# Both streams of the first feed-forward and of the key units in one matmul of 512 columns

## The chip, the cores and the metric

The kernel runs on one NeuronCore of a Trainium2 chip. The metric is the device time of one execution in microseconds (us); lower is better. Engines are named TensorE (PE in the rows, PEld for its weight loads), VectorE (DVE), ScalarE (ACT), GpSimd (POOL) and SyncE (SP).

## The reference

Two layers of a diffusion backbone work on 256 latent tokens and, in the first layer up to the attention, on 256 context tokens, each with 1024 features. What the change touches is the first feed-forward, which both streams pass with the same weights, and the keys of the attention, which both streams need:

```python
D_MODEL = 1024
SEQ = 256
...
CTX_LEN = 256
D_FF = 2816
...
def half_step_ffn(x, g_pre, g_post, shift, scale, gate, w_gate, w_up, w_down):
    h = modulated_norm(x, g_pre, shift, scale)
    y = (jax.nn.silu(h @ w_gate) * (h @ w_up)) @ w_down
    return x + FFN_RES * gate * rms_norm(y, g_post)

...
m_lat = (jax.nn.silu(c) @ w_mod[i] + b_mod[i]).reshape(b, N_MOD, 1, D_MODEL)
m_ctx = (jax.nn.silu(c_ctx) @ w_mod[i] + b_mod[i]).reshape(N_MOD, D_MODEL)
x = half_step_ffn(x, g[0], g[1], m_lat[:, 0], m_lat[:, 1], m_lat[:, 2],
                  ffn_w_gate[i, 0], ffn_w_up[i, 0], ffn_w_down[i, 0])
...
if keep_ctx:
    ctx = half_step_ffn(ctx, g[0], g[1], m_ctx[0], m_ctx[1], m_ctx[2],
                        ffn_w_gate[i, 0], ffn_w_up[i, 0], ffn_w_down[i, 0])
```

The last lines stand in the loop over the layers i, ahead of the token mixing; `keep_ctx` holds in layer 0 alone. The products `silu(c) @ w_mod` are matrix-vector products with 37.7 MB of weights for each layer; the kernel spreads them over the feed-forwards as "modulation jobs".

## The kernel before

**Layout and precision.** Features lie on the 128 partitions, tokens along the free dimension: `h` of a stream is 128 x 8 x 256 (`KT` = 8 blocks of features). Each fp32 operand is split into a rounded part and a rest (`hi`, `lo`, type float32r), and `product` (L1370 to L1374) issues three matmuls: w_hi x_hi (L1372), w_hi x_lo (L1373), w_lo x_hi (L1374). One weight unit is 128 x 1024 and makes one tile of 128 outputs: 8 blocks, 24 matmuls.

**Weight stream.** SyncE loads the units in order into 3 raw buffers. ScalarE copies each to `whi` (L434), VectorE subtracts into `wlo` (L801); both are rings of 6 units. The split of unit u + 6 waits until TensorE is done with unit u (`pe_done`).

**The first feed-forward** is 11 turns over six units each: gate and up of a tile pair s = 0, gate and up of pair s = 1, and two down units. Turns 0 and 10 are written out, 1 to 5 and 6 to 9 are loops. In a turn TensorE multiplies the four gate and up units with both streams. The latent gate and up of a pair share PSUM bank `gu[:, 0]` (gate in columns 0 to 255, up in 256 to 511), those of the context share `gu[:, 1]`. Order in a turn (`both_turn` of TensorE, L1512): (0, latent) (0, context) (1, latent) (1, context) (2, latent) (2, context), `job_sum(t)`, (3, latent) (3, context), then the two down products of the latent stream, then `job_sum(t + 1)`. Turn 0 takes both latent tiles of its first pair before the context's. After an odd latent tile the semaphore `lat_pair` rises; after each context tile `pe_done`.

ScalarE then applies SiLU to the gate half (L540), VectorE multiplies by the up half (L998). The latent result `act` is split for the down product: ScalarE `act_hi` (L544), VectorE `act_lo` (L1003). The context result goes to `act_ctx` and its down product comes after the turns, from `wstream` once more ("context down").

**Modulation jobs.** Two a turn. VectorE does a job in 8 steps, each a 128 x 512 weight block times a scalar of c, added to `part` (L816 the first, L818 the others). ScalarE rounds the total (`total_hi`, L537), VectorE subtracts (`total_lo`, L828, after a small copy to `hot`, L826), and TensorE sums over the partitions with two matmuls (`job_sum`, L1394 and L1396), for which it waits on `total_done`. All engines work strictly in the order of the program. VectorE's is set by a table in its `both_turn` (L1051): steps 0 to 3 at k = 0, 4 to 7 at k = 1, 8 to 11 at k = 2, 12 to 14 at k = 3, 15 at k = 4; each k ends with the split of unit u + k + 6, k = 2 begins with `job_lo(t)`, k = 4 ends with `job_lo(t + 1)`. At k = 1 and 3 the steps stand between the latent multiplication, `act_lo` and the context multiplication.

**After the turns** VectorE copies the latent result out of PSUM (L1140), for which the first context down product waits (`y_copied`). Later come the projection units of the attention. Units 16 to 19 are the keys, of both streams: `column_unit` once for the latent half and once for the context half of a bank, which ScalarE copies out (L659).

## Time and profile before

| | us |
|---|---|
| median of 3 runs | 1490.08 (1487.72 to 1493.79) |
| span of the profiled execution | 1499.0 |
| TensorE busy | 1434.4 (96%) |
| VectorE busy | 979.7 (65%) |
| ScalarE busy | 621.3 (41%) |
| GpSimd busy | 121.2 (8%) |
| the first feed-forward's turns | 53 to 392 us of the span |

The profiled execution is one run; its span is 8.9 us longer than the median of the runs, so a sum made from its rows is a sum of differences. A row of the timeline has start, duration, engine, line of the kernel, operation and operands; in brackets stands how long the engine was idle before it and what ended that. Matmuls are pipelined: their duration (0.28 us for 256 columns) is longer than the distance from one start to the next, so speed is read from starts. The granted clock is 1.00 at TensorE's upper level, 2.4 GHz, and 0.50 at the lower, 1.2 GHz.

### The profile page before, as it was taken

The numbers are of one execution on the slowest core, as the hardware profiler recorded it, in microseconds if no ns is written. First come the engines' busy times: TensorE is split into PE (matmuls) and PEld (weight loads), VectorE is DVE, ScalarE is ACT, GpSimd is POOL, SyncE is SP. The second block draws the span as 40 slices with busy tenths as digits, with TensorE's granted clock in tenths as the row PEclk, the third lists the DMA queues.
The fourth block names the chain that finished last, engine by engine and source line by source line (L and its number), as shares of the span: only waits on it lengthen the run. The fifth ranks groups of instructions, "written<-read, shape, count | busy, mean of one in ns | idle before, by whom it ended". The sixth has DMA issues, their size and how long they took to land.

```text
span 1499.0 us, 27870 instructions
## 1 busy us (share of the span) xinstructions
PE 1434.4 (96%) x10570; PEld 1310.5 (87%) x10570; DVE 979.7 (65%) x1425; ACT 621.3 (41%) x951; POOL 121.2 (8%) x200
## 2 busy tenths in 40 slices
PE   7899999999999999999999999999999989999997
PEld 2699999999899976589999989999876878899996
DVE  2677677777676824458787878755685785755554
ACT  2433232323465623345444455444435432544442
POOL 2000001111004002101111101100000020000000
PEclk9999999999999988999999999999999998999999
DMA  8455547777557532038888857856432432266651
GB/s 331 155 182 186 179 154 225 240 250 238 176 162 186 159 92 74 11 115 260 288 303 289 291 181 243 281 180 185 149 113 62 150 127 84 77 192 182 182 176 48
DMA packets 74482, 268.26 MB, mean 179 GB/s; under 512 B 9018, under 2 KB 9573, under 8 KB 73840
## 3 DMA queue, kind: packets, MB, share of 16 engines
q1 hardware_dynamic: 52128, 187.03, 38.4%
q0 software_dynamic: 22288, 80.30, 16.8%
q8 instruction: 47, 0.77, 0.2%
q14 instruction: 19, 0.16, 0.0%
HBM read 266.25 MB, written 1.05 MB: 178 GB/s over the span
## 4 chain that ended last, share of the span: by engine, by line
PE 68%; DVE 13%; issue 7%; ACT 6%; DMA 6%; DVEq 0%; ACTq 0%; SPq 0%; POOL 0%; POOLq 0%
PE gu L1372 13%; PE gu L1374 13%; PE gu L1373 13%; PE acc L1372 5%; PE acc L1374 5%; PE acc L1373 5%; DMA raw<-in_wstream_dram 5%; DVE wlo L801 4%; ACT whi L434 4%; PE mean_p L1414 2%; DVE part L818 1%; PE acc L1640 1%; DVE rstd L866 1%; PE gu L1481 1%; PE acc L1757 1%
## 5 line engine op out<-in xcount | busy, mean ns | idle before, releaser
L801 DVE TENSOR_TENSOR wlo<-raw,whi 128x1024 fp32r<-128x1024 f32 x350 | 432.9, 1242 | 284.4 <-ACT whi L434 282.9
L1372 PE MATMUL gu<-h_lat_hi,whi 128*128 128x256 f32 x1760 | 506.8, 288 | 11.6 <-DVE h_lat_lo L910 4.1
L434 ACT ACTIVATE whi<-raw 128x1024 fp32r<-128x1024 f32 x350 | 366.8, 1053 | 333.6 <-PE gu L1374 144.2
L1373 PE MATMUL gu<-h_lat_lo,whi 128*128 128x256 f32 x1760 | 500.1, 284 | 0.0
L1374 PE MATMUL gu<-h_lat_hi,wlo 128*128 128x256 f32 x1760 | 500.0, 284 | 0.0
L1372 PEld LDWEIGHTS gu<-h_lat_hi,whi 128*128 128x128 f32 x1760 | 339.8, 193 | 29.5 <-issue 17.7
L1373 PEld LDWEIGHTS gu<-h_lat_lo,whi 128*128 128x128 f32 x1760 | 340.0, 193 | 2.3 <-issue 1.7
L1374 PEld LDWEIGHTS gu<-h_lat_hi,wlo 128*128 128x128 f32 x1760 | 339.9, 193 | 0.0
L1372 PE MATMUL acc<-act_hi,whi 128*128 128x256 f32 x880 | 250.8, 285 | 3.3 <-DVE z L1140 2.6
L1373 PE MATMUL acc<-act_lo,whi 128*128 128x256 f32 x880 | 249.6, 284 | 0.0
L1374 PE MATMUL acc<-act_hi,wlo 128*128 128x256 f32 x880 | 249.5, 284 | 0.0
L818 DVE SCALAR_TENSOR_TENSOR part<-wm,cvec,part 128x512 f32<-128x512 f32 x266 | 199.3, 749 | 5.4
L1372 PEld LDWEIGHTS acc<-act_hi,whi 128*128 128x128 f32 x880 | 169.3, 192 | 6.2 <-DVE act_lo L1131 3.3
L1373 PEld LDWEIGHTS acc<-act_lo,whi 128*128 128x128 f32 x880 | 169.4, 193 | 0.0
L1374 PEld LDWEIGHTS acc<-act_hi,wlo 128*128 128x128 f32 x880 | 169.4, 193 | 0.0
L356 POOL DMA_DIRECT2D wm<-in_wmod_dram x136 | 71.9, 529 | 598.0 <-DVE part L818 577.9
L540 ACT ACTIVATE gated<-gu 128x256 f32<-128x256 f32 x110 | 41.9, 381 | 166.9 <-PE gu L1374 166.9
L1372 PE MATMUL gu<-h_ctx_hi,whi 128*128 128x256 f32 x384 | 108.7, 283 | 1.3 <-DVE area L998 1.3
L1373 PE MATMUL gu<-h_ctx_lo,whi 128*128 128x256 f32 x384 | 108.7, 283 | 0.0
L1374 PE MATMUL gu<-h_ctx_hi,wlo 128*128 128x256 f32 x384 | 108.6, 283 | 0.0
L998 DVE TENSOR_TENSOR act<-gated,gu 128x256 f32<-128x256 f32 x88 | 36.8, 419 | 61.5 <-ACT gated L540 61.2
L1372 PEld LDWEIGHTS gu<-h_ctx_hi,whi 128*128 128x128 f32 x384 | 73.7, 192 | 1.5 <-DVE wlo L801 1.5
(193 smaller groups left out, 1466.2 us busy)
## 6 DMA issues: line engine op xcount, KB each, us to landing
raw<-in_wstream_dram SPq DMA_DIRECT2D x350, 512.0 KB, 4.0
wm<-in_wmod_dram POOLq DMA_DIRECT2D x136, 512.0 KB, 5.1
area<-in_wmod_dram POOLq DMA_DIRECT2D x8, 512.0 KB, 8.0
area<-in_rpb_dram POOLq DMA_DIRECT2D x32, 64.0 KB, 3.1
x_lat<-in_x_in_dram SPq DMA_DIRECT2D x1, 1024.0 KB, 8.6
area<-in_ctx_in_dram SPq DMA_DIRECT2D x1, 1024.0 KB, 12.0
area<-in_dft_in_dram POOLq DMA_DIRECT2D x1, 1024.0 KB, 8.3
area<-in_window_in_dram POOLq DMA_DIRECT2D x1, 1024.0 KB, 11.4
```

The lines of the kernel that those rows point to most:

```text
L356: pool.dma_start(dst[:, 2 * part_:2 * part_ + 2, :], src[:, 2 * part_:2 * part_ + 2, :]).then_inc(sems[part_ // 2], 16)
L434: nc.scalar.activation(whi[:, phase % RING, :], raw[:, phase % RAW, :], ACT.Copy).then_inc(hi_done, 1)
L540: nc.scalar.activation(gated[:, s, :], gu[:, s, 0:T], ACT.Silu).then_inc(silu_done, 1)
L801: nc.vector.tensor_tensor(wlo[:, u.base % RING, :], raw[:, u.base % RAW, :], whi[:, u.base % RING, :].bitcast(F32), ALU.subtract).then_inc ...
L818: ins = nc.vector.scalar_tensor_tensor(out=part[:, :], in0=wm[:, kt, :], scalar=c, in1=part[:, :], op0=ALU.mult, op1=ALU.add)
L866: nc.vector.reciprocal(rstd[:, :], root[:, :]).then_inc(rstd_done, 1)
L998: nc.vector.tensor_tensor(dst, gated[:, s, :], gu[:, s, T:2 * T], ALU.mult).then_inc(act_mul, 1)
L1372: nc.tensor.matmul(out_, w_hi, x_hi, start=start, stop=False, skip_group_check=True)
L1373: nc.tensor.matmul(out_, w_hi, x_lo, start=False, stop=False, skip_group_check=True)
L1374: return nc.tensor.matmul(out_, w_lo, x_hi, start=False, stop=stop, skip_group_check=True)
L1414: ins = nc.tensor.matmul(mean_p[:, 0:T], mean_mat[:, :], sq[:, m, :], start=(m == 0), stop=(m == KT - 1))
L1481: ins = nc.tensor.matmul([job_p, gu[:, 0, :]][l % 2][0:2, :], cvec[:, kt, :], src[:, kt, :], start=(kt == 0), stop=(kt == KT - 1))
```

## The change

The two streams' `h` move into one tensor of 128 x 8 x 2 x 256, so that a feature block of both streams is one run of 512 columns. Bank `gu[:, 0]` now holds the gate of both streams, `gu[:, 1]` the up of both. From turn 1 on (and for the second pair of turn 0) a weight block is multiplied with both streams in one matmul of 512 columns. ScalarE applies SiLU to 512 columns at once, after the gate tile. VectorE waits for the up tile's `pe_done`, multiplies for the latent and then for the context stream, does `act_lo`, and then the job steps of that k. The semaphore `lat_pair` is gone. The key units take one matmul of 512 columns in place of two of 256.

```diff
@@ tensors
-        h_hi = [sb("h_lat_hi", [P, KT, T], F32R), sb("h_ctx_hi", [P, KT, T], F32R)]
-        h_lo = [sb("h_lat_lo", [P, KT, T], F32R), sb("h_ctx_lo", [P, KT, T], F32R)]
+        both_hi = sb("h_hi", [P, KT, 2, T], F32R)
+        both_lo = sb("h_lo", [P, KT, 2, T], F32R)
+        h_hi = [both_hi[:, :, s, :] for s in (LAT, CTX)]
+        h_lo = [both_lo[:, :, s, :] for s in (LAT, CTX)]
@@ ScalarE
+            def both_turn(u, n, ft, t):
+
+                for k in range(6):
+                    s = (k // 2) % 2
+                    if k in (0, 2):
+                        a.wait_ge(pe_done, at_unit(u, k + 1))
+                        if not (isinstance(ft, int) and ft + s == 0):
+                            a.wait_ge(act_mul, 2 * s + n)
+                        nc.scalar.activation(gated[:, :, :].rearrange("p a b -> p (a b)"), gu[:, 0, :],
+                                             ACT.Silu).then_inc(silu_done, 1)
+                    if k in (1, 3):
+                        a.wait_ge(act_mul, 2 * s + n + 1)
+                        nc.scalar.activation(act_hi[:, s, :], act[:, s, :], ACT.Copy).then_inc(act_hi_done, 1)
+                    split(u.plus(k + RING))
+                    if k in (1, 4):
+                        job_hi(t if k == 1 else t + 1)
@@ VectorE, both_turn
-                def latent(s, ops):
-                    gate_up(n + 2 * s, 0, act[:, s, :])
-                    for x in ops[:2]:
-                        op(x)
-                    act_los(n + 2 * s, ft + s, s)
-                    for x in ops[2:]:
-                        op(x)
-
-                first = isinstance(i, int) and i == 0
                 for k in range(6):
                     s = (k // 2) % 2
                     ops = plan.get(k, ())
-                    if k == 0 and first:
-                        latent(0, ops)
-                    elif k in (1, 3):
-                        if not (k == 1 and first):
-                            latent(s, ops)
+                    if k == 2:
+                        job_lo(t, r)
+                    if k in (1, 3):
+                        v.wait_ge(silu_done, ft + (s + 1))
+                        v.wait_ge(pe_done, at_unit(u, k + 1))
+                        nc.vector.tensor_tensor(act[:, s, :], gated[:, 0, :], gu[:, 1, 0:T], ALU.mult).then_inc(act_mul, 1)
                         dst = act_ctx[:, ft + s, :] if isinstance(ft, int) \
                             else act_ctx[:, bass.ds(ft + s, 1), :].rearrange("p a b -> p (a b)")
-                        gate_up(n + (2 * s + 1), 1, dst)
...
+                        nc.vector.tensor_tensor(dst, gated[:, 1, :], gu[:, 1, T:2 * T], ALU.mult).then_inc(act_mul, 1)
+                        act_los(n + 2 * s, ft + s, s)
+                    for x in ops:
+                        op(x)
                     split(u.plus(k + RING))
@@ TensorE, both_turn
+                def tile(k):
+                    s = k // 2
+                    pe.wait_ge(lo_done, at_unit(u.plus(k), 1))
+                    if k % 2 == 0:
+                        pe.wait_ge(silu_done, ft + s)
+                    else:
+                        pe.wait_ge(act_mul, n + 2 * s)
+                    for kt in range(KT):
+                        ins = product(gu[:, k % 2, :], *wblock(u.plus(k), kt), both_hi[:, kt, :, :], both_lo[:, kt, :, :],
+                                      kt == 0, kt == KT - 1)
+                    ins.then_inc(pe_done, 1)
+
+                if first:
+                    for k, stream in ((0, LAT), (1, LAT), (0, CTX), (1, CTX)):
+                        stream_tile(k, stream)
+                else:
+                    tile(0)
+                    tile(1)
+                tile(2)
                 job_sum(t, first)
-                tile(3, LAT)
-                tile(3, CTX)
+                tile(3)
@@ TensorE, key units
-                column_unit(Unit(U_AB + idx), gu[:, idx % 2, 0:T], lat, last=False)
-                column_unit(Unit(U_AB + idx), gu[:, idx % 2, T:2 * T], con)
+                column_unit(Unit(U_AB + idx), gu[:, idx % 2, :], (both_hi, both_lo))
```

`stream_tile`, used for the first pair of turn 0 alone, is the old tile of one stream with the new places in the banks. The table of the job steps is the same.

What this does to the order of the instructions is best seen on VectorE. First its first pair in a turn, up to the job that TensorE's first `job_sum` waits for (turn 10, which is written out; L998, L1003, L818, L801, L828 of before are L1069 and L1072, L1005, L820, L803, L830 of after). Before:

```order
L998 TENSOR_TENSOR act<-gated,gu 128x256 [waits silu_done]
L818 SCALAR_TENSOR_TENSOR part<-wm,cvec,part 128x512 [waits gemv_step,wm_landed1]
L818 SCALAR_TENSOR_TENSOR part<-wm,cvec,part 128x512 [waits gemv_step]
L1003 TENSOR_TENSOR act_lo<-act,act_hi 128x256 [waits act_mul,act_hi_done]
L818 SCALAR_TENSOR_TENSOR part<-wm,cvec,part 128x512 [waits gemv_step] x2
L998 TENSOR_TENSOR area<-gated,gu 128x256 [waits silu_done]
L801 TENSOR_TENSOR wlo<-raw,whi 128x1024 [waits hi_done]
L826 CAST hot<-one_in 128x22 [waits total_hi_done]
L828 TENSOR_TENSOR total_lo<-part,total_hi 128x512
```

The same place on VectorE after the change:

```order
L1069 TENSOR_TENSOR act<-gated,gu 128x256 [waits pe_done,silu_done]
L1072 TENSOR_TENSOR area<-gated,gu 128x256
L1005 TENSOR_TENSOR act_lo<-act,act_hi 128x256 [waits act_mul,act_hi_done]
L820 SCALAR_TENSOR_TENSOR part<-wm,cvec,part 128x512 [waits gemv_step,wm_landed1]
L820 SCALAR_TENSOR_TENSOR part<-wm,cvec,part 128x512 [waits gemv_step] x3
L803 TENSOR_TENSOR wlo<-raw,whi 128x1024 [waits hi_done]
L828 CAST hot<-one_in 128x22 [waits total_hi_done]
L830 TENSOR_TENSOR total_lo<-part,total_hi 128x512
```

The two job steps that stood ahead of `act_lo`, and the two ahead of the context's multiplication, now stand behind both multiplications and `act_lo`, and the first multiplication waits for `pe_done` of the up tile.

Next, on VectorE, the second pair of the same turn, up to the job of the last `job_sum`. Before:

```order
L998 TENSOR_TENSOR act<-gated,gu 128x256 [waits silu_done]
L818 SCALAR_TENSOR_TENSOR part<-wm,cvec,part 128x512 [waits gemv_step,wm_landed1]
L818 SCALAR_TENSOR_TENSOR part<-wm,cvec,part 128x512 [waits gemv_step]
L1003 TENSOR_TENSOR act_lo<-act,act_hi 128x256 [waits act_mul,act_hi_done]
L818 SCALAR_TENSOR_TENSOR part<-wm,cvec,part 128x512 [waits gemv_step]
L998 TENSOR_TENSOR area<-gated,gu 128x256 [waits silu_done]
L801 TENSOR_TENSOR wlo<-raw,whi 128x1024 [waits hi_done]
L818 SCALAR_TENSOR_TENSOR part<-wm,cvec,part 128x512 [waits gemv_step]
L801 TENSOR_TENSOR wlo<-raw,whi 128x1024 [waits hi_done]
L826 CAST hot<-one_in 128x22 [waits total_hi_done]
L828 TENSOR_TENSOR total_lo<-part,total_hi 128x512
```

After, on the same engine:

```order
L1069 TENSOR_TENSOR act<-gated,gu 128x256 [waits pe_done,silu_done]
L1072 TENSOR_TENSOR area<-gated,gu 128x256
L1005 TENSOR_TENSOR act_lo<-act,act_hi 128x256 [waits act_mul,act_hi_done]
L820 SCALAR_TENSOR_TENSOR part<-wm,cvec,part 128x512 [waits gemv_step,wm_landed1]
L820 SCALAR_TENSOR_TENSOR part<-wm,cvec,part 128x512 [waits gemv_step] x2
L803 TENSOR_TENSOR wlo<-raw,whi 128x1024 [waits hi_done]
L820 SCALAR_TENSOR_TENSOR part<-wm,cvec,part 128x512 [waits gemv_step]
L803 TENSOR_TENSOR wlo<-raw,whi 128x1024 [waits hi_done]
L828 CAST hot<-one_in 128x22 [waits total_hi_done]
L830 TENSOR_TENSOR total_lo<-part,total_hi 128x512
```

Here three job steps move behind the multiplications in the same way; what follows them is unchanged. On TensorE `job_sum` keeps its place between tiles 2 and 3 and at the turn's end.

## Rows read from the trace of the kernel before

**Rows 1.** From 60 to 360 us: PE, PEld, DVE, ACT, POOL busy, clock, DMA.

```profile
60.00:360.00 300.00, 294.57 (x2392) 286.53 (x2391) 220.65 (x326) 98.69 (x145) 29.43 (x56) 1.00 0.62 201
```

**Rows 2.** Waits of TensorE, 60 to 392 us: total, times, longest.

```profile
PE job_p L1394 <- DVE total_lo L828: 4.1, 12, 1.6
```

**Rows 3.** Timeline of TensorE (start, duration, line, operation): 256 and 512 columns.

```profile
362.13 0.28 PE L1372 MATMUL gu<-h_lat_hi,whi 128*128 128x256 f32 x1
...
367.88 0.28 PE L1372 MATMUL gu<-h_lat_hi,whi 128*128 128x256 f32 x1
...
575.75 0.39 PE L1622 MATMUL acc<-whi,h_lat_hi 128*128 128x512 f32 x1
...
583.23 0.39 PE L1622 MATMUL acc<-whi,h_ctx_hi 128*128 128x512 f32 x1
```

**Rows 4.** Timeline of TensorE: start of turn 1, end of turn 2, start of turn 3.

```profile
89.66 0.28 PE L1372 MATMUL gu<-h_lat_hi,whi 128*128 128x256 f32 x1
...
149.59 0.41 PE L1394 MATMUL job_p<-total_hi,hot 128*22 128x512 f32 x1 [0.21 <-DVE total_lo L828]
150.16 0.38 PE L1372 MATMUL gu<-h_lat_hi,whi 128*128 128x256 f32 x1
```

**Rows 5.** Timeline of VectorE in turn 3, first pair and its job.

```profile
159.51 0.42 DVE L998 TENSOR_TENSOR act<-gated,gu 128x256 f32<-128x256 f32 x1 [0.98 <-ACT gated L540]
...
161.30 0.42 DVE L1003 TENSOR_TENSOR act_lo<-act,act_hi 128x256 fp32r<-128x256 f32 x1
161.64 1.53 DVE L818 SCALAR_TENSOR_TENSOR part<-wm,cvec,part 128x512 f32<-128x512 f32 x2
...
163.42 1.22 DVE L801 TENSOR_TENSOR wlo<-raw,whi 128x1024 fp32r<-128x1024 f32 x1
...
164.63 0.69 DVE L828 TENSOR_TENSOR total_lo<-part,total_hi 128x512 fp32r<-128x512 f32 x1
```

**Rows 6.** Timeline of VectorE in turn 3, second pair and its job.

```profile
171.49 0.42 DVE L998 TENSOR_TENSOR act<-gated,gu 128x256 f32<-128x256 f32 x1 [1.44 <-ACT gated L540]
...
177.92 1.23 DVE L801 TENSOR_TENSOR wlo<-raw,whi 128x1024 fp32r<-128x1024 f32 x1 [0.72 <-ACT whi L434]
...
179.14 0.68 DVE L828 TENSOR_TENSOR total_lo<-part,total_hi 128x512 fp32r<-128x512 f32 x1
```

**Rows 7.** Timeline of ScalarE in turn 3.

```profile
159.97 0.42 ACT L544 ACTIVATE act_hi<-act 128x256 fp32r<-128x256 f32 x1 [0.49 <-DVE act L998]
...
177.79 0.61 ACT L537 ACTIVATE total_hi<-part 128x512 fp32r<-128x512 f32 x1
```

**Rows 8.** Timeline of VectorE, then TensorE, in turn 0.

```profile
67.02 0.41 DVE L998 TENSOR_TENSOR act<-gated,gu 128x256 f32<-128x256 f32 x1
...
71.79 3.11 DVE L818 SCALAR_TENSOR_TENSOR part<-wm,cvec,part 128x512 f32<-128x512 f32 x4
...
76.82 0.49 DVE L816 TENSOR_SCALAR part<-wm,cvec 128x512 f32<-128x512 f32 x1
...
67.58 0.36 PE L1372 MATMUL gu<-h_lat_hi,whi 128*128 128x256 f32 x1 [0.47 <-DVE act L998]
...
76.77 0.41 PE L1394 MATMUL job_p<-total_hi,hot 128*22 128x512 f32 x1 [1.64 <-DVE total_lo L828]
...
77.25 0.28 PE L1372 MATMUL gu<-h_lat_hi,whi 128*128 128x256 f32 x1
```

**Rows 9.** End of turn 10: VectorE, then TensorE.

```profile
391.07 0.69 DVE L828 TENSOR_TENSOR total_lo<-part,total_hi 128x512 fp32r<-128x512 f32 x1
...
392.72 1.23 DVE L801 TENSOR_TENSOR wlo<-raw,whi 128x1024 fp32r<-128x1024 f32 x1 [0.96 <-ACT whi L434]
...
395.03 0.36 PE L1372 MATMUL acc<-act_hi,whi 128*128 128x256 f32 x1 [2.57 <-DVE z L1140]
```

**Rows 10.** Short stretches, as rows 1; third number from the end: granted clock.

```profile
76.00:78.00 2.00, 1.23 (x9) 1.06 (x10) 1.86 (x5) 0.51 (x1) 0.00 (x0) 1.00 0.27 25
...
396.00:400.00 4.00, 4.00 (x21) 3.88 (x20) 1.12 (x3) 2.42 (x6) 0.00 (x0) 0.57 0.28 111
```

More of the change, by code:

```diff
@@ L285, in program @@
         total_split, total_done = sem("total_hi_done"), sem("total_lo_done")
-        lat_pair, y_copied = sem("latent_pair_done"), sem("y_copied")
+        y_copied = sem("y_copied")
         cs_ready = sem("cs_ready")
@@ L1513, in both_turn, with stream_tile @@
                 t = i * 2 + T_AHEAD
-                def tile(k, stream):
-                    s = (k // 2) % 2
-                    uk = u.plus(k)
-                    if stream == LAT or first:
-                        pe.wait_ge(lo_done, at_unit(uk, 1))
-                    if k % 2 == 0 and not (first and k == 0):
-                        pe.wait_ge(act_mul, n + (2 * s + stream - 1))
+                def stream_tile(k, stream):
+                    if stream == LAT:
+                        pe.wait_ge(lo_done, at_unit(u.plus(k), 1))
                     for kt in range(KT):
-                        if first and k == 0 and kt % 2 == 0:
+                        if k == 0 and kt % 2 == 0:
                             pe.wait_ge(h_ready, 4 * stream + kt // 2 + 1)
-                        ins = product(gu[:, stream, (k % 2) * T:(k % 2) * T + T], *wblock(uk, kt),
+                        ins = product(gu[:, k, stream * T:stream * T + T], *wblock(u.plus(k), kt),
                                       h_hi[stream][:, kt, :], h_lo[stream][:, kt, :], kt == 0, kt == KT - 1)
@@ L1528, in tile @@
                         ins.then_inc(pe_done, 1)
-                    elif k % 2:
-                        ins.then_inc(lat_pair, 1)
-                start = [(0, LAT), (1, LAT), (0, CTX), (1, CTX)] if first else \
-                    [(0, LAT), (0, CTX), (1, LAT), (1, CTX)]
-                for k, stream in start + [(2, LAT), (2, CTX)]:
-                    tile(k, stream)
+                def tile(k):
+                    s = k // 2
+                    pe.wait_ge(lo_done, at_unit(u.plus(k), 1))
+                    if k % 2 == 0:
[13 more added lines that the diff above has]
+                tile(2)
                 job_sum(t, first)
-                tile(3, LAT)
-                tile(3, CTX)
+                tile(3)
                 for s in range(2):
```

39 lines of the change are left out of this document (8 added, 31 removed).

## The prediction, made before the changed kernel was run

> **What bounds the kernel now.** I read the chain of waits first: TensorE's products of this one helper carry it. Then I read the stretch that the change touches, the loop of the first feed-forward. From 60 to 360 us TensorE is busy for 294.57 of 300 us at a granted clock of 1.00, VectorE for 220.65 [rows 1]. From the waits of TensorE in the same stretch the reader should take one name: what it waits for is `total_lo`, the last step of a modulation job on VectorE, 12 times and 4.1 us in all [rows 2]. So TensorE's stream sets the pace, but one chain of VectorE lies directly beneath it. VectorE is idle a quarter of the time, and an idle share tells nothing of whether its work lies in the right place.
>
> A turn lasts 30.27 us: the first product of turn 1 starts at 89.66 and that of turn 10 at 362.13, nine turns [rows 3, 4].
>
> **What the wide matmul saves.** 48 matmuls of 256 columns take from 362.13 to 367.88, so 0.1198 us from start to start [rows 3]. 512 columns with weights of the same size are in the trace too, in the projection of the values: 33 of them from 575.75 to 583.23, 0.2267 us each [rows 3]. A pair of narrow ones becomes one wide one, 0.2396 against 0.2267: 0.0129 us saved. A weight tile of both streams (24 wide matmuls) takes 5.44 us in place of 5.75. Ten turns of four tiles, two tiles in turn 0 and the four key units make 46 tiles, 1104 pairs, 14.2 us of TensorE time.
>
> The Trainium skill (TensorE: Matmul & The Clock Gate, "Wait — 56ns, not 53.3ns?") has 215.7 ns from start to start for 512 columns and a fixed 2.5 ns for each matmul. The trace does not agree: it shows 226.7 ns for 512 [rows 3]. By the page the three tiles that stand in a turn's path below would be 0.79 us shorter, and the whole sum +3.9 us instead of +12.3 (the nine turns, tile 3 of turn 0 and the key units).
>
> **What the change moves.** Before, the latent stream had its own bank with gate and up; its half of a pair was complete 2.87 us before the context half, and SiLU, multiplication and split of it ran beneath the context's matmuls. VectorE got two job steps done between. Now the up tile of both streams ends at one moment. VectorE waits there for `pe_done`, multiplies twice, waits for ScalarE's `act_hi`, subtracts, and only then come the job steps, which are queued behind that wait. TensorE, one tile later, waits for the job's `total_lo`. I put the clock at zero at the first matmul of a steady turn.
>
> *First half.* Gate and up tile of pair 0: 2 x 5.44 = 10.88. The last matmul ends 0.39 - 0.23 = 0.16 later [rows 3]; I take 0.10 for the signal: 0.04 lies between a multiplication's end and `act_hi` (159.51 + 0.42 against 159.97) [rows 5, 7], and the loop's waits on registers may add a little (estimate). VectorE multiplies at 11.14. ScalarE's `act_hi` starts 0.46 later (159.51 to 159.97) and takes 0.42 [rows 5, 7], so with 0.04 for the signal the subtraction starts at 12.06; the second multiplication fits beneath. The next instruction starts 0.34 after it (161.30 to 161.64) [rows 5]: 12.40. Four job steps take 3.11, less 0.08 that neighbours overlap, 3.03 [rows 8]: 15.43. Split of a unit and `hot`: from 163.42 to 164.63, 1.21 [rows 5]: 16.64. `total_lo` 0.69 [rows 5] and 0.05 to the matmul (the same kind of signal): 17.38. ScalarE's `total_hi`, 0.61 [rows 7], lies beneath the split. TensorE is done with tile 2 at 16.32 and would go on at 16.44. It waits 0.94 us.
>
> *Second half.* From the job's first matmul to the next tile 0.48 (76.77 to 77.25) [rows 8]: tile 3 from 17.86 to 23.30. The same 0.16 + 0.10: 23.56. To the first job step 0.92 + 0.34: 24.82. Three steps 2.24: 27.06 (four steps less one of 0.79). Split 1.15 (1.23 less 0.08 [rows 6]): 28.21. The last job step, 0.75 less 0.08: 28.88. Split and `hot` 1.22 (177.92 to 179.14) [rows 6]: 30.10. `total_lo` and signal: 30.84. TensorE has finished both down products at 23.30 + 5.75 = 29.05, and waits 1.67 us behind the 0.12 of passage. Then 0.57 to the first matmul of the next turn (149.59 to 150.16) [rows 4]: 31.41.
>
> The wait of before at this place, 0.21 us [rows 4], had another cause: VectorE was 0.72 us idle there for ScalarE's `whi` [rows 6], which waited for the first down product. That cause is gone; VectorE's own queue takes its place.
>
> So a turn takes 31.4 in place of 30.27, **+1.14 us, nine times: +10.3 us.** The 1.24 us that a turn's wide matmuls save are spent, and as much again.
>
> *Turn 0.* It has no latent half ahead of VectorE's splits. Before, VectorE is done with them at 67.02 [rows 8]. Now follow four job steps, the first a plain product of 0.49 and not 0.75 [rows 8], so 2.76, to 69.78; split 1.15; then the chain as above: 1.26, 3.03, 1.21, 0.74, to 77.17. Before, the job matmul started at 76.77 [rows 8]: +0.4. The old waits of 0.47 and 1.34 us before tile 2 are gone, but all of that gain is waited for in front of the job. From there to turn 1: 13.9 (31.41 - 17.38, less 0.1 for the loop's branch) against 12.89 (76.77 to 89.66) [rows 4, 8]: +1.0. Together +1.4 us.
>
> *The clock in turn 0.* Tile 2 now starts at 66.95 and its last matmul ends at 72.55, so TensorE is idle for 4.6 us. The trace shows the granted clock after 2.57 us of idle time before 395.03: a mean of 0.58 from 396 to 400, so most of it at the lower of the two levels, 1.2 GHz, which costs 4 x 0.42 = 1.7 us [rows 9, 10]. After 1.64 us of idle time before 76.77 it stayed at 1.00 [rows 8, 10]. So 4.6 us will let it fall, once: **+1.7 us**.
>
> *Turn 10 and after.* Its `total_lo` ends 1.0 us later than before, counted from its start (30.7, against 391.07 + 0.69 - 362.13 = 29.63) [rows 3, 9]. Behind it VectorE was idle for 0.96 us for ScalarE's `whi`, which waited for the second down product [rows 9]; that product is now long done. So the copies of the latent result, for which TensorE waits until 395.03, come 1.0 us sooner after `total_lo`. Sum +0.1 us.
>
> *The key units.* Four tiles, 96 pairs, with nothing behind them on VectorE but splits: -1.2 us, whole on the path. ScalarE copies the finished bank beneath the next unit as before. One SiLU of 512 columns in place of two of 256, and the two-part rows of h, lie on engines with idle time: nothing, unless ScalarE were late for a split, and `total_hi` above has 0.6 us to spare. The weight stream keeps three raw buffers and the same order; the turn becomes longer, so the transfers have more time.
>
> **Sum:** +10.3 + 1.4 + 1.7 + 0.1 - 1.2 = +12.3 us. The profiled execution's span is 1499.0, 8.9 above the median 1490.1 of the runs; every term is a difference of a few us, so I add it to the median: **1502.4 us.**
>
> **Rivals.**
>
> *TensorE stays the bound (faster).* Place: the first `job_sum` and the second of each turn. It decides at the first half's chain, 6.50 us from the up tile's end (10.88) to the job's matmul (17.38), against 5.56 of tile 2 with its passage; the second needs 7.54 (23.30 to 30.84) against 5.87. If VectorE needed 0.94 us less in the one and 1.67 in the other, the whole 14.2 us would come, and most of turn 0's waits: 1475 us. The order of VectorE's instructions speaks against it, as does that the old chain had nothing left at the end of a turn (the wait of 0.21). 4%.
>
> *The chains are shorter than I make them, or the clock does not fall in turn 0.* Half the signal times and no fall give +8 to +3: 1493 to 1498. The terms are sums of starts in the same loop, so an error of 0.3 us in a turn is as much as I allow. 10%.
>
> *The clock falls in every turn.* The idle stretch at each turn's end is 1.6 us and one of 0.9 lies 12 us before it. If each such stretch brought 1.7 us at the lower clock, nine or ten times, the time would be 1519. Against it: 1.64 us in turn 0 did not let it fall [rows 8, 10]; for it: the new one is as long, ten times over, and 2.57 sufficed. 9%. The Trainium skill (same page, "A second HAM failure mode: psum-queue depth-cycling") tells of a kernel of 512-column matmuls going round PSUM banks whose short idle times made the clock swing; no row here shows it for idle times this short.
>
> *The wide matmul does not do what it says.* If 512 columns of h as the moving side took twice 0.1198, the three tiles in a turn's path would be 0.31 longer each: +8.4 us, and the key units' 1.2 lost: 1512. The only row of 512 has the weight matrix as the moving side. 3%.
>
> **How the numbers follow.** Forecast 74%, its own range 1498 to 1507 (0.3 us a turn each way, and the clock). The range of 1494 to 1511 takes in most of the shorter chains and a clock that falls in a few turns. 0.5% is 7.5 us, about what a measurement can tell here. Faster by more: 5%. Within it: 13%, the shorter chains. Slower: 82%.
>
> **What would show it.** In the changed kernel the waits of TensorE for `total_lo` should rise from 4.1 to about 31 us in this stretch, some 0.9 and 1.6 us by turns, and the first of them near 4.6. The turn should read 31.4 us. VectorE should show its idle time before the first multiplication of a pair and none from there to `total_lo`. The granted clock should dip once near 76 to 82 us. Wrong would be: no waits at `job_sum` (rival one), a clock below 1.00 throughout the stretch (rival three), wide matmuls 0.24 us apart (rival four).

## The result and the profile after

The changed kernel takes 1508.94 us (median of 4 runs, 1504.10 to 1515.68) against 1491.44 (1487.72 to 1493.79) of the kernel before on the same chip: a ratio of 1.0108, 95% interval 1.0081 to 1.0136, or 16.1 us more (12.1 to 20.3) by that ratio; the two medians lie 17.5 us apart. Predicted were 12.3 us more. A second measurement on another chip (`changed_again`, below) gave 1.0127 (1.0081 to 1.0173).

The busy time of each engine over the same stretch as [rows 1] and the waits of TensorE as in [rows 2]. Columns of the first: stretch, length, busy time and count of PE, PEld, DVE, ACT, POOL, granted clock, DMA share, GB/s.

```profile
60.00:360.00 300.00, 273.32 (x1402) 227.75 (x1401) 206.33 (x306) 88.61 (x118) 26.41 (x50) 0.98 0.56 189
75.00:83.00 8.00, 4.64 (x12) 3.47 (x13) 7.15 (x10) 2.06 (x3) 1.05 (x2) 0.57 0.40 115
284.00:288.00 4.00, 4.00 (x12) 3.18 (x11) 2.73 (x5) 0.00 (x0) 1.05 (x2) 0.57 0.96 329
```

The waits of TensorE for `total_lo` from 60 to 420 us, to the end of turn 10 as in [rows 2] (engine, line, what it waited for: total us, times, longest):

```profile
PE job_p L1383 <- DVE total_lo L830: 31.7, 22, 4.7
```

TensorE's busy time fell by 21 us in 300, and that is not work saved: the engine stands still instead, for 26.7 us of the 300. What it waits for is one name, `total_lo`, 31.7 us in place of 4.1. The two short stretches of a lower clock are new.

TensorE's timeline: turn 0's first job, the start of turn 1, the second job of turn 1 and both jobs of turn 2 (start, duration, line, operands; in brackets the idle time and what ended it):

```profile
73.26 0.39 PE L1363 MATMUL gu<-h_hi,wlo 128*128 128x512 f32 x1
78.36 0.62 PE L1383 MATMUL job_p<-total_hi,hot 128*22 128x512 f32 x1 [4.71 <-DVE total_lo L830]
...
94.31 0.39 PE L1361 MATMUL gu<-h_hi,whi 128*128 128x512 f32 x1
94.54 0.39 PE L1362 MATMUL gu<-h_lo,whi 128*128 128x512 f32 x1
94.76 0.39 PE L1363 MATMUL gu<-h_hi,wlo 128*128 128x512 f32 x1
...
125.20 0.41 PE L1383 MATMUL job_p<-total_hi,hot 128*22 128x512 f32 x1 [1.62 <-DVE total_lo L830]
...
143.33 0.41 PE L1383 MATMUL job_p<-total_hi,hot 128*22 128x512 f32 x1 [0.93 <-DVE total_lo L830]
...
156.78 0.41 PE L1383 MATMUL job_p<-total_hi,hot 128*22 128x512 f32 x1 [1.61 <-DVE total_lo L830]
157.03 0.40 PE L1385 MATMUL job_p<-total_lo,hot 128*22 128x512 f32 x1
157.34 0.49 PE L1361 MATMUL gu<-h_hi,whi 128*128 128x512 f32 x1
157.68 0.40 PE L1362 MATMUL gu<-h_lo,whi 128*128 128x512 f32 x1
```

The wide matmuls do start 0.227 us apart (94.31, 94.54, 94.76), as [rows 3] had it for other operands. In turns 1 to 9 the first job waits 0.92 to 0.93 us and the second 1.61 to 1.62. A turn lasts 31.6 us (125.20 to 156.78, the second jobs of turns 1 and 2) against 30.27.

VectorE in turn 2, first pair, to set beside [rows 5]:

```profile
133.22 1.22 DVE L803 TENSOR_TENSOR wlo<-raw,whi 128x1024 fp32r<-128x1024 f32 x1 [4.18 <-ACT whi L436]
137.00 0.42 DVE L1069 TENSOR_TENSOR act<-gated,gu 128x256 f32<-128x256 f32 x1 [2.55 <-PE gu L1363]
137.33 0.41 DVE L1072 TENSOR_TENSOR area<-gated,gu 128x256 f32 x1
138.01 0.43 DVE L1005 TENSOR_TENSOR act_lo<-act,act_hi 128x256 fp32r<-128x256 f32 x1 [0.26 <-ACT act_hi L575]
138.35 3.11 DVE L820 SCALAR_TENSOR_TENSOR part<-wm,cvec,part 128x512 f32<-128x512 f32 x4
141.38 1.22 DVE L803 TENSOR_TENSOR wlo<-raw,whi 128x1024 fp32r<-128x1024 f32 x1
142.51 0.17 DVE L828 CAST hot<-one_in 128x22 fp32r x1
142.59 0.68 DVE L830 TENSOR_TENSOR total_lo<-part,total_hi 128x512 fp32r<-128x512 f32 x1
```

VectorE stands idle for 2.55 us (and 4.18 us before the split ahead of it) while four job steps, which wait for nothing of TensorE in the order shown above, are queued behind the multiplication. From 138.35 on it has no gap, and TensorE waits for its end.

Outside the stretch, the first and the next operation after the key units' products:

```profile
543.85 0.79 PE L1361 MATMUL gu<-h_hi,whi 128*128 128x512 f32 x1 [3.13 <-DVE h_lo L912]
...
568.04 1.12 PE L1594 MATMUL gu<-area 64*128 64x512 f32 x2 [0.69 <-ACT area L661]
```

24.19 us, against 25.46 before (525.28 to 550.74): 1.27 us less. In both the clock was at its lower level for some 3 us of it; two traces without a fall there give the difference more cleanly (under keys_only).

The profiled spans, 1506.1 and 1499.0, differ by 7.1 us only, less than the medians do. The reason lies outside the change: in the 60 us after the key units the granted clock was 0.77 in the profiled execution of before and 1.00 in that of after, with the same kind of products (173 matmuls in it against 222). Before, then after:

```profile
550.00:610.00 60.00, 57.13 (x173) 33.20 (x173) 21.25 (x44) 20.25 (x40) 14.87 (x20) 0.77 0.27 63
```

```profile
567.00:627.00 60.00, 57.13 (x222) 34.26 (x221) 27.40 (x62) 25.53 (x52) 15.10 (x20) 1.00 0.26 66
```

Before, the clock stood at its lower level for 27.3 of these 60 us, which is 13.7 us of full speed. It fell there in six of the twelve executions whose traces are used here, at a loss of 3.4 to 13.7 us, in changed and unchanged kernels alike. So one pair of spans is no measure of a change of 10 us; the stages are compared by their own rows, the whole by medians.

### The profile page after: what moved, and what is told of

The parts are those of the page before. It is cut to its first block, busy times and chain, and to the rows that moved or that the text cites. A ratio compares the mean times of both kernels' runs of the same rounds, so it can differ in the third digit from the quotient of the medians.

```text
span 1506.1 us, 25678 instructions
## 1 busy us (share of the span) xinstructions
PE 1415.3 (94%) x9466; PEld 1249.6 (83%) x9466; DVE 978.1 (65%) x1425; ACT 616.3 (41%) x929; POOL 121.0 (8%) x200
## 4 chain that ended last, share of the span: by engine, by line
PE 63%; DVE 18%; issue 8%; ACT 6%; DMA 4%; DVEq 0%; ACTq 0%; POOL 0%; SPq 0%; POOLq 0%
PE gu L1361 12%; PE gu L1363 12%; PE gu L1362 12%; DVE wlo L803 5%; PE acc L1361 5%; PE acc L1362 5%; PE acc L1363 5%; DVE part L820 5%; DMA raw<-in_wstream_dram 4%; ACT whi L436 2%; PE mean_p L1403 2%; PE job_p L1470 1%; DVE rstd L868 1%; DVE total_lo L830 1%; PE acc L1636 1%
## 5 line engine op out<-in xcount | busy, mean ns | idle before, releaser
L803 DVE TENSOR_TENSOR wlo<-raw,whi 128x1024 fp32r<-128x1024 f32 x350 | 432.2, 1240 | 266.4 <-ACT whi L436 265.2
L1361 PE MATMUL gu<-h_hi,whi 128*128 128x256 f32 (+1 forms) x1776 | 552.8, 311 | 11.7 <-DVE h_lo L912 7.2
L1362 PE MATMUL gu<-h_lo,whi 128*128 128x256 f32 (+1 forms) x1776 | 545.5, 307 | 0.0
L1363 PE MATMUL gu<-h_hi,wlo 128*128 128x256 f32 (+1 forms) x1776 | 545.2, 307 | 0.0
L1361 PEld LDWEIGHTS gu<-h_hi,whi 128*128 128x128 f32 x1776 | 342.6, 193 | 43.8 <-issue 17.7
L1362 PEld LDWEIGHTS gu<-h_lo,whi 128*128 128x128 f32 x1776 | 342.6, 193 | 16.4 <-issue 1.7
L1363 PEld LDWEIGHTS gu<-h_hi,wlo 128*128 128x128 f32 x1776 | 342.3, 193 | 14.9
L820 DVE SCALAR_TENSOR_TENSOR part<-wm,cvec,part 128x512 f32<-128x512 f32 x266 | 199.4, 750 | 6.2
L1403 PE MATMUL mean_p<-sq,mean_mat 128*128 128x256 f32 x240 | 58.3, 388 | 11.8 <-ACT sq L473 11.3
L1403 PEld LDWEIGHTS mean_p<-sq,mean_mat 128*128 128x128 f32 x240 | 43.4, 190 | 24.8 <-issue 13.1
L542 ACT ACTIVATE gated<-gu 128x256 f32<-128x256 f32 x66 | 25.1, 380 | 91.0 <-PE gu L1363 91.0
L868 DVE RECIPROCAL rstd<-root 128x256 f32<-128x256 f32 x15 | 26.3, 1750 | 48.1 <-ACT root L479 48.1
## 6 DMA issues: line engine op xcount, KB each, us to landing
area<-in_ctx_in_dram SPq DMA_DIRECT2D x1, 1024.0 KB, 11.6
```

What stands on the lines that cost most here:

```text
L542: nc.scalar.activation(gated[:, s, :], gu[:, s, 0:T], ACT.Silu).then_inc(silu_done, 1)
L803: nc.vector.tensor_tensor(wlo[:, u.base % RING, :], raw[:, u.base % RAW, :], whi[:, u.base % RING, :].bitcast(F32), ALU.subtract).then_inc ...
L820: ins = nc.vector.scalar_tensor_tensor(out=part[:, :], in0=wm[:, kt, :], scalar=c, in1=part[:, :], op0=ALU.mult, op1=ALU.add)
L868: nc.vector.reciprocal(rstd[:, :], root[:, :]).then_inc(rstd_done, 1)
L1361: nc.tensor.matmul(out_, w_hi, x_hi, start=start, stop=False, skip_group_check=True)
L1362: nc.tensor.matmul(out_, w_hi, x_lo, start=False, stop=False, skip_group_check=True)
```

## Experiments

The theory is that VectorE's order makes the waits; the job steps stand behind the wait for the up tile, and the wide matmuls themselves keep their price. The rivals are that the wide matmuls or their single bank cost the time, or that the clock does. "From the first product to context down" is the stretch from TensorE's first product of this feed-forward to the first product of context down: 342.07 us before (52.96 to 395.03), 358.67 after (54.18 to 412.85). The length of a loop turn is the mean of the nine from the start of turn 1 to that of turn 10: 30.27 us before. In the changed kernel it is 31.73 with one fall of the clock in it (at 284 us) and 31.57 in `changed_again`, where the clock stayed up; 31.57 is used below.

### steps_early: the same kernel, the steps ahead of the wait

```diff
-                plan = {0: (0, 1, 2, 3), 1: (4, 5, 6, 7), 2: (8, 9, 10, 11), 3: (12, 13, 14), 4: (15,)}
+                plan = {0: (0, 1, 2, 3, 4, 5, 6, 7), 2: (8, 9, 10, 11, 12, 13, 14, 15)}
```

> The changed kernel with one line of its table of job steps different: steps 0 to 7 at k = 0 and 8 to 15 at k = 2, so that VectorE does them while TensorE still works on the pair, and behind the wait for the up tile stand only the two multiplications, act_lo and the split. Theory (VectorE's order makes the waits): the 0.93 us at the first job_sum goes and the 1.61 us at the second falls to about 0.2, so a turn reads 28.9 to 29.2 us in place of 31.57, and the kernel is some 12 us faster than the one before: 1476 to 1482. Turn 0 keeps its long wait (three job steps more or less, about 4 to 5 us). Rival (the wide matmuls, their single bank of gate and up, or the multiplication's wait on the whole up tile are what costs): the turn stays near 31.5 us and the time near 1508.

Measured: 1485.25 us, ratio 0.9948 (0.9925 to 0.9970). Waits of TensorE for the jobs, and the two jobs of a turn:

```profile
PE job_p L1383 <- DVE total_lo L830: 8.0, 12, 5.5
```

```profile
167.20 0.39 PE L1383 MATMUL job_p<-total_hi,hot 128*22 128x512 f32 x1
...
179.22 0.41 PE L1383 MATMUL job_p<-total_hi,hot 128*22 128x512 f32 x1 [0.21 <-DVE total_lo L830]
```

Both waits went as expected: none at the first job, 0.21 at the second, a turn of 29.03 us. One line of a table turns a loss of 1.1% into a gain of 0.5%. The time is 3 us above what I gave: turn 0 took 38.94 us (36.70 before) with a wait of 5.52, and the wait before context down rose from 2.57 to 3.54, with 2.9 us of full speed lost to the clock behind it, in place of 1.7.

### old_steps_late: the order alone, with narrow matmuls

```diff
@@ VectorE, both_turn of the kernel before
                 def latent(s, ops):
                     gate_up(n + 2 * s, 0, act[:, s, :])
-                    for x in ops[:2]:
-                        op(x)
                     act_los(n + 2 * s, ft + s, s)
-                    for x in ops[2:]:
-                        op(x)
...
                         gate_up(n + (2 * s + 1), 1, dst)
+                        for x in ops:
+                            op(x)
```

> The kernel before, with its narrow matmuls, banks and semaphores, and only VectorE's job steps at k = 1 and k = 3 moved behind act_lo and behind the context's multiplication, where the changed kernel has them. Theory: the order alone costs time without any wide matmul; from the durations of the rows the first job_sum should wait 0 to 0.1 us and the second 1.0 to 1.3, a turn of 31.2 to 31.4 us in place of 30.27, about +10 us on the kernel before: 1497 to 1503. Rival (the slowdown comes from the wide matmuls themselves): a turn of 30.3 us and no difference.

Measured: 1505.35 us, ratio 1.0088 (1.0069 to 1.0106). The stretch from the first product to context down is 354.88 us, 12.8 more than before. TensorE's jobs in its trace, the second one of turn 1 and the first of turn 2:

```profile
122.31 0.41 PE L1391 MATMUL job_p<-total_hi,hot 128*22 128x512 f32 x1 [1.16 <-DVE total_lo L828]
...
140.59 0.41 PE L1391 MATMUL job_p<-total_hi,hot 128*22 128x512 f32 x1
```

No matmul is wide, and a turn lasts 31.52 us, as long as in the changed kernel. The first job starts 0.3 us later in its turn than before (17.67 against 17.37), the second another 0.96. My 31.2 to 31.4 was slightly low, and with it the time: 13 us more than the kernel before by the ratio, where I had given about 10. The slowdown is there without any wide matmul; that rival falls.

### narrow_steps_early: the fourth corner

The kernel before with the table of steps_early.

> The kernel before, with its narrow matmuls, and the table of steps_early (steps 0 to 7 at k = 0, 8 to 15 at k = 2). It is the fourth corner beside the kernel before, old_steps_late and steps_early. Theory (a turn is TensorE's stream plus what VectorE's order makes it wait): in steps_early 0.21 us remained at the second job_sum, the same as before, so here a turn should stay at 30.2 to 30.3 us; turn 0 may lose 0 to 2 us; 1489 to 1496, no difference to the kernel before. The gain of steps_early (29.06 against 30.27 a turn) is then the width's alone, 96 x 0.0129 = 1.24. Rival (the new order gives a gain of its own, whatever the width): a turn below 30.0 us and some 3 us or more gained.

Measured: 1499.84 us, ratio 1.0040 (1.0014 to 1.0066). Turns of 30.26 us, as expected. The total was a miss: turn 0 took 40.62 us in place of 36.70. Its waits:

```profile
PE gu L1372 <- DVE area L998: 4.6, 1, 4.6
```

With one stream at a time, the context's multiplication stands behind the latent one's steps, and in turn 0 the whole of steps 0 to 7 now lies between the two. That is the changed kernel's mistake in small, in another place. The waits of turn 0 grew by 1.6 us only (4.56 in place of 1.34 and 1.64); the clock fell with the long one, stood at its lower level from 74.81 to 81.64 us, and most of the 3.9 us is this.

The four corners, loop turns in us:

| | job steps late | job steps early |
|---|---|---|
| narrow matmuls | 31.52 | 30.26 |
| wide matmuls | 31.57 | 29.03 |

In the early column TensorE sets the turn, and the width is worth 1.23 us, against 96 x 0.0129 = 1.24. In the late column a chain on VectorE does, and the width is worth nothing. That is a balance of two things. Up to the ends of the two up tiles the wide turn is 1.12 us shorter (10.78 and 5.70 us in place of 11.49 and 6.11, to the start of the tile's last matmul). But its chains from there to the job are 1.14 us longer (6.76 and 7.75 in place of 6.18 and 7.19), since the latent stream's `act_hi` and `act_lo` no longer run beneath the context's matmuls.

### first_half_early: a dose

```diff
-                plan = {0: (0, 1, 2, 3), 1: (4, 5, 6, 7), 2: (8, 9, 10, 11), 3: (12, 13, 14), 4: (15,)}
+                plan = {0: (0, 1, 2, 3, 4, 5, 6, 7), 2: (8, 9, 10, 11), 3: (12, 13, 14), 4: (15,)}
```

> The changed kernel with steps 0 to 7 at k = 0, the second half's table untouched: a dose between the changed kernel and steps_early. Theory: the wait at the first job_sum (0.93 us) goes, the one at the second stays at 1.6, since tile 3's end, not the first job, starts its chain; turn 30.6 us, about 1498 to 1502. Rival (the two waits are one chain, so that taking out the first only makes the second longer): the second grows to 2.5 us and the turn stays at 31.5.

Measured: 1498.37 us, ratio 1.0034 (1.0013 to 1.0055); turns of 30.43 us. The waits of TensorE for the jobs:

```profile
PE job_p L1383 <- DVE total_lo L830: 23.3, 12, 5.5
```

The first wait is gone from the loop turns, the second stays at 1.61 to 1.62; the 5.5 is that of turn 0's first job. The two waits are separate: each chain starts at the end of its own up tile, as the prediction had it. The turn is 1.14 us shorter and not 0.93 (I had given 30.6), because the idle time in brackets counts from a matmul's modelled end: from the last matmul of tile 2 to the job's it was 1.32 us with the wait (142.01 to 143.33) and 0.23 without (110.34 to 110.57), a difference of 1.09.

### keys_only

The kernel before with `h` in one tensor and 512 columns in the key units alone.

> The kernel before with h of both streams in one tensor and only the four key units with 512 columns; the turns keep their narrow matmuls. Its time is not to be told from the kernel before; what counts is the stretch from the first to the last product of the key units in the trace, 25.46 us before. Theory: 24.2 us (96 x 0.0129 = 1.24 less), and turns of 30.27 us as before, so that the new layout of h costs nothing where the products stay narrow. Rival: the two-part rows of h slow its writers or TensorE's reads, and a turn or the start of the first product (52.96) is 0.3 us or more later.

Measured: one execution, 1485.92 us. The key units take 24.36 us (527.74 to 552.10), 1.10 less than before, and turns last 30.27 us. Both stretches hold a fall of the clock, of the same length. In the two traces in which it stayed up there, the narrow key units take 23.97 us (`old_steps_late`) and the wide ones 22.76 (`turn0_filled`), so 1.21 less. With a fall twice as long the wide ones took 25.63 (`changed_again`), so this stretch can be compared only at an equal clock. The first product came at 53.63 against 52.96. It lies between 53.10 and 54.18 in all the other kernels with either layout (53.69 and 53.27 in narrow ones with the old layout), so 52.96 was the odd one and the layout does not explain it. No cost of the layout is to be seen where the products stay narrow.

### turn0_filled, turn0_filled20, changed_again: what the clock's fall costs

```diff
                 tile(2)
+                if first:
+                    pe.wait_ge(act_mul, 2)
+                    for _ in range(38):
+                        nc.tensor.matmul(gu[:, 1, 0:P], mean_mat[:, :], mean_mat[:, :], start=True, stop=True)
                 job_sum(t, first)
```

turn0_filled20 has 20 in place of 38; changed_again is the changed kernel once more.

> The changed kernel with 38 extra matmuls (128 columns, results thrown away) in turn 0 between tile 2 and job_sum, where TensorE waited 4.7 us. Nothing of the result depends on them. Theory (the idle time makes the granted clock fall, two stretches at the lower level from 75 to 83 us, 3.4 us lost): the clock stays at 1.00 from 60 to 90 us, turn 1 starts 36.5 to 37.0 us after the first product in place of 40.1. The waits of the later turns stay at 0.93 and 1.61, so the time falls by those 3.4 us only: 1502 to 1508. Rival (the fall is not tied to this wait, but comes at some distance from the fall at 52 to 59 us): the clock dips all the same.

Measured: 1507.25 us, ratio 1.0105 (1.0063 to 1.0147). The clock stayed up, but the extra matmuls took twice what I had reckoned with, since each is recorded as two of 0.11 us (timeline of TensorE in turn 0):

```profile
73.06 8.64 PE L1538 MATMUL gu<-mean_mat 128*128 128x128 f32 x76
81.46 0.47 PE L1383 MATMUL job_p<-total_hi,hot 128*22 128x512 f32 x1
```

The job started 3.9 us after `total_lo` had ended (77.52), turn 0 took 42.07 us (expected 36.5 to 37.0), and the saving was spent. So I made a second try, on one chip with the changed kernel itself.

> turn0_filled with 20 extra matmuls in place of 38: the trace of turn0_filled shows one of them as two passes of 0.11 us, 8.4 us for 38, so they ran 3.7 us past the total they should bridge, and turn 0 took 42.07 us though the clock stayed at 1.00. 20 of them take 4.4 us, 0.3 us less than the wait. Theory (the clock falls because of the idle stretch): granted clock 1.00 from 60 to 90 us, turn 1 starts 36.6 to 37.1 us after the first product (40.13 in the changed kernel), and the time is 2 to 5 us below changed_again. Rival: the clock falls later instead, at a wait of the loop, and nothing is gained.

> The changed kernel itself, on the same chip as turn0_filled20, so that the two can be set against each other and its size against the kernel before is known better. Expected: a ratio of 1.008 to 1.013 again; in the trace the two waits of 0.93 and 1.61 us in every turn, and about one of ten of the 1.61 us waits followed by a stretch of the clock at the lower level (so far 1 of 10 in the changed kernel, 2 of 10 in turn0_filled, 0 of 10 in first_half_early).

Measured: turn0_filled20 1507.29 us, ratio 1.0079 (1.0046 to 1.0111); changed_again 1513.94, ratio 1.0127 (1.0081 to 1.0173). The granted clock in turn 0, first of turn0_filled20, then of changed_again:

```profile
60.00:90.00 30.00, 29.13 (x201) 26.75 (x199) 25.15 (x40) 13.05 (x18) 2.09 (x4) 1.00 0.45 149
```

```profile
75.00:83.00 8.00, 5.25 (x13) 3.97 (x14) 6.54 (x10) 2.06 (x3) 1.06 (x2) 0.62 0.42 131
```

With the idle stretch filled the clock stays at 1.00, and turn 0 takes 38.12 us, against 40.90 in changed_again and 40.13 in the changed kernel before. So the fall costs 2.0 to 2.8 us there. It is not the 3.4 that I had subtracted for the expectation of 36.6 to 37.1, which missed: the clock is low from 75 us on, and until 78 TensorE waits anyway. What is left, 38.12 - 36.70 = 1.4 us, is the chain on VectorE alone. In the medians the two intervals overlap, so the 6.6 us between them are not shown by the times; the traces show the 2 to 3. In the loop of turn0_filled20 the clock fell once all the same, at 154.6 us.

### reordered and reordered2: the order fitted to the wide matmuls

```diff
@@ VectorE: steps of a job right behind each other, its total split right behind them
+                plan = {1: (0, 1, 2, 3, 4, 5, 6, 7), 3: (8, 9, 10, 11, 12, 13, 14, 15)} if first else \
+                    {0: (0, 1, 2, 3, 4, 5, 6, 7), 2: (8, 9, 10, 11, 12, 13, 14, 15)}
...
-                    if k == 2:
+                    if k == (2 if first else 1):
                         job_lo(t, r)
...
-                    if k == 4:
+                    if k == (4 if first else 2):
                         job_lo(t + 1, r + 1)
@@ ScalarE: job_hi behind the splits of k = 0 and 2 (turn 0: 2 and 4)
@@ TensorE: the second job's sum one tile into the next turn
                     tile(0)
+                    job_sum(t - 1)
                     tile(1)
...
-                job_sum(t + 1)
+                if stop:
+                    job_sum(t + 1)
```

> The changed kernel with the whole order of the turn fitted to it: steps 0 to 7 at k = 0 and 8 to 15 at k = 2 (turn 0: k = 1 and 3), the jobs' totals split right behind them, job_sum(t) between tiles 2 and 3 as before and the second job's job_sum one tile into the next turn, so that no total is waited for. Nothing of the computation changes. Theory: no wait at any job_sum, a turn of 28.8 to 29.0 us, no long wait in turn 0 and so no fall of the clock there (granted clock 1.00 from 60 to 280 us); the 14 us of TensorE time come whole, and some of turn 0's old waits: 1468 to 1475, faster than both kernels. Rival (another wait stands beneath: ScalarE's gate of 512 columns, or the bank of gu that the next pair's gate tile needs): TensorE waits 0.3 to 1 us for silu_done or act_mul in each turn, 1478 to 1485.

Measured: 1479.31 us, ratio 0.9902 (0.9885 to 0.9920). In turn 0 the first job's sum stands behind tile 3 (not shown in the diff), so nothing is waited for before it. No loop turn has a wait from turn 2 on; they last 28.45 us. The clock stayed at 1.00 through turn 0, which took 30.97 us. But the median missed my range by 4 us and lies where I had put the rival, though the rival's waits, for `silu_done` or `act_mul`, are not in the trace. All waits of TensorE from 50 to 420 us:

```profile
PE acc L1370 <- DVE z L1138: 3.3, 1, 3.3
PE gu L1370 <- DVE h_lo L989: 2.8, 1, 2.8
PE job_p L1392 <- DVE total_lo L833: 2.8, 1, 2.8
PE acc L1370 <- DVE act_lo L1008: 1.3, 1, 1.3
```

The second was there before. The third and fourth are in turn 1, and ScalarE's timeline shows where they begin:

```profile
81.79 1.06 ACT L436 ACTIVATE whi<-raw 128x1024 fp32r<-128x1024 f32 x1 [1.50 <-PE acc L1372]
...
94.34 1.06 ACT L436 ACTIVATE whi<-raw 128x1024 fp32r<-128x1024 f32 x1 [7.97 <-DMA raw<-in_wstream_dram]
```

A unit's load had not landed: in turn 0 VectorE freed its raw buffer only behind eight job steps, by the split that starts at 85.62 us. The first, before context down, is a split of the last unit ahead of the copies that TensorE waits for. reordered2 moves both; in turn 0 it also puts steps 12 to 15 behind the split of k = 4, and at the end of turn 10 the context's first `act_hi` and `act_lo` go ahead of the last split.

```diff
@@ VectorE, turn 0, second pair
                         act_los(n + 2 * s, ft + s, s)
+                    if first and k == 3:
+                        split(u.plus(2 + RING))
+                        split(u.plus(3 + RING))
                     for x in ops:
                         op(x)
@@ VectorE and ScalarE, end of turn 10
-                    split(u.plus(k + RING))
+                    if not (last and k == 5):
+                        split(u.plus(k + RING))
...
                                       acc[:, c, :]).then_inc(y_copied, 1)
+            split(Unit(U_CD - 1 + RING))
```

> reordered with two places mended. In turn 0 VectorE does the splits of units 8 and 9 ahead of steps 8 to 15 and that of unit 10 in their middle, so that the raw buffers come free 5 us sooner and the load of unit 11, for which ScalarE waited 7.97 us until 94.3, is landed in time. At the end of turn 10 the split of the turn's last unit moves behind the context's first act_hi and act_lo and behind the copies of the latent result. Theory: the waits of 2.77 and 1.25 us in turn 1 with their clock fall of 1.7, and the 3.29 us before context down (0.3 to 0.8 remain) with the clock fall at 378 to 386 (3.4), go: 9 to 12 us less than reordered, 1467 to 1472. Rival: the loads in turn 1 are late because the transfers themselves are at their limit there (DMA busy share 0.93 from 90 to 95 us), so that only the second place helps: 1472 to 1476.

Measured: 1471.65 us (1465.17 to 1478.24), ratio 0.9855 (0.9819 to 0.9892), the fastest of all: 21.6 us below the kernel before by the ratio, 21.0 by the medians. Waits:

```profile
PE gu L1380 <- DVE h_lo L991: 2.8, 1, 2.8
PE acc L1380 <- DVE act_lo L1010: 1.9, 1, 1.9
PE job_p L1402 <- DVE total_lo L835: 0.5, 1, 0.5
PE acc L1380 <- DVE z L1147: 0.4, 1, 0.4
```

The stretch from the first product to context down is 321.28 us, 20.8 less than before: 5.3 in turn 0 (31.40 against 36.70; the second job's sum, some 0.5 us, now counts to turn 1), 12.1 in the nine turns (eight of them last 28.45, turn 1 still 32.81), 3.4 behind the start of turn 10. The wait before context down is 0.4 in place of 3.3, and turn 1 keeps one of 1.9 with a fall of the clock behind it. Against reordered, turns 0 and 1 together are 1.9 us shorter and the stretch behind the start of turn 10 is 2.9 shorter. That is 4.8 us by the traces and some 7 by the ratios, less than the 9 to 12 that I had given. So both places were real: that split now starts at 79.95, and ScalarE no longer waits for the unit's load. What is left in turn 1 comes from VectorE: TensorE waits for its `act_lo` (112.43), which stands behind eight job steps.

## Why the prediction was right, point by point

**What bounds the kernel.** Right: TensorE before, and one chain of VectorE directly beneath. The two by two table shows it: with the same wide matmuls the turn is 29.03 or 31.57 by the place of a turn's job steps alone.

**The saving of the wide matmul, 0.0129 us a pair.** Right. steps_early against narrow_steps_early gives 1.23 us a turn for 96 pairs. The starts of wide matmuls lie 0.227 us apart (94.31, 94.54, 94.76). The 215.7 ns of the Trainium skill (TensorE: Matmul & The Clock Gate, "Wait — 56ns, not 53.3ns?"), by which the sum would have been +3.9, are not what runs here.

**First half of a turn, wait 0.94.** Measured 0.93. The multiplication came 11.21 us after the turn's first matmul (125.79 to 137.00; predicted 11.14), `act_lo` 1.01 behind it (0.92), the job matmul at 17.54 (17.38). TensorE was late by some 0.13 itself (0.1 of it because the first matmul of a turn takes 0.34 us to the next one's start, 157.34 to 157.68, and not 0.23), so the wait stayed the same and the turn became longer. That the wait came out within 0.01 is in part luck, since both sides of it were late.

**Second half, wait 1.67.** Measured 1.61; from job matmul to job matmul 13.45 us (143.33 to 156.78), predicted 13.46.

**The nine turns, +10.3.** The steady loop was undersized: 31.57 a turn against 31.41. The nine turns of changed_again, in which the clock stayed up, took 284.10 us (94.47 to 378.57) against 272.47 before: +11.6. The missing 0.16 us a turn is the two pieces just named, both in the first half. The multiplication came 0.07 late: TensorE's own matmuls took 0.13 more, and the signal, estimated at 0.10, only 0.04 (136.57 + 0.39 to 137.00). And `act_lo` came 0.09 later behind it than the rows of turn 3 of before had it.

**Turn 0, +1.4.** With the clock held up, turn0_filled20 measured +1.4 (38.12 against 36.70). Right; in the changed kernel the job waited 4.71, predicted 4.6, and in turn0_filled20 it started 24.18 us after the first product, predicted 24.21.

**The clock in turn 0, +1.7.** The mechanism was right, the size too small: 2.0 and 2.8. The clock was low for 6.8 us, from 75.9 to 82.7, longer than the 4 us of [rows 10] that I had taken. (Those rows read 0.57, not 0.58; the 1.7 does not change.)

**Turn 10 and after, +0.1.** Measured +0.05: from the first product of turn 10 to that of context down 32.97 us (379.88 to 412.85) against 32.90.

**The key units, -1.2.** Measured -1.27, -1.10 in keys_only, and -1.21 between the two traces in which the clock stayed up there.

**The sum.** 11.6 + 1.4 + 2.4 + 0.05 - 1.21 = 14.2 us (2.4 is the middle of 2.0 and 2.8), and in some executions a fall of the clock in the loop (1.7 us; once in the changed kernel, at 284, not in changed_again). The measured 16.1 (12.1 to 20.3) holds both that and the predicted 12.3, and does not tell them apart. What I had sized too small were the first half of a turn and the length of the clock's fall, both by less than the range.

**The rivals.** TensorE as the bound: the order of VectorE's queue decided against it. steps_early makes it nearly true in the loop by changing nothing but that order; reordered and reordered2, which also move work on ScalarE and TensorE, make it true there. Shorter chains: the turn was longer by 0.16. The clock in every turn: behind the second job's wait it fell in 4 of the 50 turns of five traces, so this rival was wrong as I put it, but not nothing. The width not saving: fell with the rows above.

## What to carry to other kernels

When two short instructions become one long one, all that used to run beneath the second now waits for the end of the whole. Work that does not depend on that end must be moved ahead of the wait on its own engine in the same edit; an engine that is idle for a quarter of the time can still be late if its queue is in the wrong order. Whether the bound has moved is quickly seen by undoing the suspected cause alone, in both versions: a table of two by two told more than any single time.

## What the runs showed of the hardware

The granted clock fell after shorter idle stretches of TensorE than I had expected, and not always. In the stretch from 60 us to context down, over all the kernels here, it fell in or right behind each of the 13 idle stretches of 1.91 us and longer. Behind the last waits of the turns, 1.6 us each (turns 0 to 9 of the changed kernel, changed_again, first_half_early, turn0_filled and turn0_filled20), it fell 4 times in 50. Behind two such stretches with 0.6 us of work between (the end of turn 10 in the same five) it fell 4 times in 5. In old_steps_late it fell behind two of 1.02 and 1.83 at the same place. Behind 1.34 and 1.64 us with 3.1 us of work between (turn 0 of before and of keys_only) it did not fall. Waits of 0.93 us were never followed by a fall. A fall took 1.7 or 3.4 us of TensorE's full speed with it, and what it cost the kernel was less where TensorE waited during it. Over the whole of an execution the lower level took between 17 and 35 us of full speed in the twelve traces, more than half of it after 430 us, behind the stretch that was changed. In the runs of one kernel a longer time goes with a lower mean clock (turn0_filled: 1504.07 us at 0.989, 1515.91 at 0.982), by more than most of the terms argued over here.

A float32 matmul of 128 columns whose operands are not of the rounded type is recorded as two matmuls of 0.11 us (76 for 38 in 8.64 us), which a filler has to be sized by.
